# Linear heads of a hybrid decoder block: output kept with tokens on the partitions, then turned

## The reference

```python
# q_dec, a, v, s_prev: of one head; chunks n of 64 tokens
o = o_intra + jnp.einsum('bhnck,bhnkv->bhncv', q_dec, s_prev)      # o_intra = a @ v_c
o = o.transpose(0, 2, 3, 1, 4).reshape(bsz, s, A_HEADS, A_DV)      # 4 heads, 128 values each
o = o * lax.rsqrt(jnp.mean(o * o, axis=-1, keepdims=True) + EPS)   # per token and head
o = o.reshape(bsz, s, A_WIDTH) * norm_g.astype(f32) * jax.nn.silu(g.astype(f32))
```

## Time and profile before

| | us |
|---|---|
| median of 3 runs | 2257.88 (2255.01 to 2258.12) |
| the profiled execution | 2253.26 |
| its span in the trace | 2251.3 |
| PE busy | 2207.8 (98%), 11144 matmul instructions |
| DVE busy | 1438.0 (64%) |
| ACT busy | 1002.2 (45%) |
| POOL busy | 439.0 (19%) |

### The profile page before, as it was taken

One profiled execution on the slowest core, in us unless ns is written; L12 is line 12 of the kernel. 1 busy time (PEld: TensorE's weight loads), 2 busy tenths in 40 slices (PEclk: granted clock), 3 DMA queues, 4 the chain that ended last, 5 costly groups with the idle time before them and its releaser, 6 DMA issues.

```text
span 2251.3 us, 30000 instructions
## 1 busy us (share of the span) xinstructions
PE 2207.8 (98%) x11144; PEld 1840.7 (82%) x11144; DVE 1438.0 (64%) x2170; ACT 1002.2 (45%) x1717; POOL 439.0 (19%) x344
## 2 busy tenths in 40 slices
PE   7999999999999999999999999999999999999997
PEld 6888888888888888878888887888888888887886
DVE  5775577657776677675576765567665655555555
ACT  5554455445553554444433333346533333333444
POOL 1231022201220122032223331000222222210000
PEclk9999999999999999999999999999999999999999
DMA  4222333233233323633345656788443332327766
GB/s 124 92 76 71 117 113 94 95 103 119 74 122 99 113 62 107 207 112 114 117 171 200 223 199 211 255 268 264 163 145 103 101 110 99 112 77 237 229 206 215
DMA packets 260705, 321.81 MB, mean 143 GB/s; under 512 B 17232, under 2 KB 168784, under 8 KB 259536
## 3 DMA queue, kind: packets, MB, share of 16 engines
q1 hardware_dynamic: 259984, 317.79, 42.9%
q10 hardware_dynamic: 576, 2.10, 0.2%
HBM read 242.76 MB, written 77.07 MB: 142 GB/s over the span
## 4 chain that ended last, share of the span: by engine, by line
PE 91%; DVE 3%; DMA 2%; ACT 1%; issue 1%; SPq 0%; POOL 0%; DVEq 0%; ACTq 0%; POOLq 0%
PE M L1157 9%; PE M L1159 9%; PE M L1158 9%; PE M L850 8%; PE M L852 8%; PE M L851 8%; PE M L1184 3%; PE X L1184 3%; PE X L1186 3%; PE X L1185 3%; PE X L1159 3%; PE X L1157 3%; PE X L1158 3%; PE M L1186 3%; PE M L1185 3%; PE M L965 2%
## 5 line engine op out<-in xcount | busy, mean ns | idle before, releaser
L2139 DVE TENSOR_TENSOR ring_lo<-ring_raw,ring_hi 128x1024 fp32r<-128x1024 f32 x154 | 189.6, 1232 | 170.3 <-ACT ring_hi L1588 169.9
L1685 DVE TENSOR_TENSOR wlo<-raw,whi 128x1024 fp32r<-128x1024 f32 x120 | 154.6, 1288 | 213.6 <-ACT whi L1220 213.4
L850 PE MATMUL M<-uhi,whi 128*128 128x512 f32 (+1 forms) x720 | 285.2, 396 | 3.7 <-DVE wlo L1685 2.1
L852 PE MATMUL M<-uhi,wlo 128*128 128x512 f32 (+1 forms) x720 | 278.2, 386 | 0.0
L851 PE MATMUL M<-ulo,whi 128*128 128x512 f32 (+1 forms) x720 | 277.8, 386 | 0.0
L1588 ACT ACTIVATE ring_hi<-ring_raw 128x1024 fp32r<-128x1024 f32 x154 | 163.3, 1060 | 234.2 <-DMA ring_raw<-a_scr 230.8
L1157 PE MATMUL M<-t_hi,wu_hi 128*128 128x512 f32 x616 | 240.4, 390 | 4.1 <-DVE gq L2055 2.3
L1159 PE MATMUL M<-t_hi,wu_lo 128*128 128x512 f32 x616 | 240.0, 390 | 0.0
L1158 PE MATMUL M<-t_lo,wu_hi 128*128 128x512 f32 x616 | 239.7, 389 | 0.0
L1220 ACT ACTIVATE whi<-raw 128x1024 fp32r<-128x1024 f32 x120 | 126.8, 1056 | 220.7 <-PE M L852 170.0
L2023 DVE TENSOR_TENSOR wu_lo<-fraw,wu_hi 128x512 fp32r<-128x512 f32 x132 | 127.6, 975 | 120.1 <-ACT wu_hi L1529 119.8
(11 more groups left out here) (281 smaller groups left out, 5081.4 us busy)
## 6 DMA issues: line engine op xcount, KB each, us to landing
raw<-in_w_in_dram SPq DMA_DIRECT2D x88, 512.0 KB, 3.8
ring_raw<-a_scr SPq DMA_DIRECT2D x154, 256.0 KB, 3.5
fraw<-in_w_gate_dram SPq DMA_DIRECT2D x44, 512.0 KB, 4.4
fraw<-in_w_up_dram SPq DMA_DIRECT2D x44, 512.0 KB, 4.8
a_scr<-au SPq DMA_DIRECT2D x88, 256.0 KB, 2.3
ring_raw<-t_scr SPq DMA_DIRECT2D x88, 256.0 KB, 3.0
ring_raw<-in_w_down_dram SPq DMA_DIRECT2D x66, 256.0 KB, 3.0
raw<-in_w_out_dram SPq DMA_DIRECT2D x32, 512.0 KB, 3.8
```

The costliest lines, as they stand in the source:

```text
L850: mm(bank, whi[s][:, kb, :], hi, start=first, stop=False)
L852: return mm(bank, wlo[s][:, kb, :], hi, start=False, stop=last)
L1685: V.tensor_tensor(wlo[s][:, :, :], raw[s][:, :, :], whi[s][:, :, :].bitcast(F32), ALU.subtract).then_inc(s_lo[s], 1)
L2139: V.tensor_tensor(lo[:, :, :], raw_r[:, :, :], hi[:, :, :].bitcast(F32), ALU.subtract).then_inc(s_rowlo, 1)
```

## The change

The output is now made with tokens on the partitions. In OUTPUT the operands of all twelve products change places: `amask` and a 64-token piece of `qdec` are held, `iv` and the state are streamed. A chunk's product so writes 64 partitions by 128 columns, where it wrote 128 by 64. ACT squares X[2] in four pieces and sums each along the row into `oss`; the root and the reciprocal follow as before. DVE then multiplies X[2] by the reciprocal, spread along the row by its access pattern, into `sqo`, and this is now what reports `s_y1`. PE turns `sqo` into X[3] (`head_turn`, in the place of `head_mul`), and DVE multiplies X[3] by `ga` and the gate in one instruction. The sums of ones and the spreading by PE are gone, and so is the multiplication of X[2] by the gate in OUTPUT.

```diff
@@ PE
             def output(it, a):
                 for b in range(TB):
-                    mm(X[2][:, b * P:(b + 1) * P], iv[:, b * P:(b + 1) * P], amask[:, b, :],
+                    mm(X[2][:, b * P:(b + 1) * P], amask[:, b, :], iv[:, b * P:(b + 1) * P],
...
-                    last = mm(X[2][:, n * CHUNK:(n + 1) * CHUNK], before,
-                              qdec[a % 2][:, n * CHUNK:(n + 1) * CHUNK],
+                    b, c = divmod(n, 2)
+                    last = mm(X[2][CHUNK * c:CHUNK * c + CHUNK, b * P:(b + 1) * P],
+                              qdec[a % 2][:, n * CHUNK:(n + 1) * CHUNK], before,
-            def head_sum(it, a):
-                pe.wait_ge(s_sq, it * HEADS + a + 1)
-                pe.wait_ge(s_st, it * NCH * HEADS + NCH * a + NCH)
-                sums(X[3], sqo, s_asum)
-
-            def head_mul(it, a):
-                pe.wait_ge(s_arr, it * HEADS + a + 1)
-                spread(X[3], hrnrm, s_amul)
+            def head_turn(it, a):
+                pe.wait_ge(s_y1, it * HEADS + a + 1)
+                for b in range(TB):
+                    last = tr(X[3][:, b * P:(b + 1) * P], sqo[:, b * P:(b + 1) * P], ident[:, :])
+                last.then_inc(s_amul, 1)
@@ ACT
             def output(it, a):
                 act.wait_ge(s_o, it * HEADS + a + 1)
...
-                A(sqo[:, :], X[2][:, :], ACT.Square).then_inc(s_sq, 1)
+                for b in range(TB):
+                    tokens = slice(b * P, (b + 1) * P)
+                    A(sqo[:, tokens], X[2][:, tokens], ACT.Square, accum_out=oss[:, b:b + 1]).then_inc(s_sq, 1)
             def head_sum(it, a):
-                act.wait_ge(s_asum, it * HEADS + a + 1)
+                act.wait_ge(s_sq, (it * HEADS + a + 1) * TB)
...
-                A(hnrm[:, :], X[3][:, 0:TB], ACT.Sqrt, scale=1.0 / P, bias=epst[:, 0:1]).then_inc(s_aroot, 1)
+                A(hnrm[:, :], oss[:, :], ACT.Sqrt, scale=1.0 / P, bias=epst[:, 0:1]).then_inc(s_aroot, 1)
@@ DVE
-            def output(it, a):
-                n = it * HEADS + a
-                dve.wait_ge(s_sq, n + 1)
-                dve.wait_ge(s_gs, n + 1)
-                V.scalar_tensor_tensor(out=gate[a % 2][:, :], in0=X[2][:, :], scalar=ga[:, a:a + 1],
-                                       in1=gate[a % 2][:, :], op0=ALU.mult, op1=ALU.mult).then_inc(s_y1, 1)
             def head_sum(it, a):
                 dve.wait_ge(s_aroot, n + 1)
...
                 V.reciprocal(hrnrm[:, :], hnrm[:, :]).then_inc(s_arr, 1)
+                dve.wait_ge(s_arr, n + 1)
+                V.tensor_tensor(sqo[:, :].rearrange("p (b v) -> p b v", b=TB),
+                                X[2][:, :].rearrange("p (b v) -> p b v", b=TB),
+                                hrnrm[:, :].rearrange("p (b o) -> p b o", o=1).broadcast_to([P, TB, P]),
+                                ALU.mult).then_inc(s_y1, 1)
             def head_mul(it, a):
                 dve.wait_ge(s_amul, n + 1)
-                dve.wait_ge(s_y1, n + 1)
-                V.tensor_tensor(gate[a % 2][:, :], gate[a % 2][:, :], X[3][:, :], ALU.mult).then_inc(s_ya, 1)
+                dve.wait_ge(s_gs, n + 1)
+                V.scalar_tensor_tensor(out=gate[a % 2][:, :], in0=X[3][:, :], scalar=ga[:, a:a + 1],
+                                       in1=gate[a % 2][:, :], op0=ALU.mult, op1=ALU.mult).then_inc(s_ya, 1)
```

More of the change, by code:

```diff
@@ L251, in block_program @@
         nrm = sb("nrm", [P, TB]); rnrm = sb("rnrm", [P, TB])
-        hnrm = sb("hnrm", [P, TB]); hrnrm = sb("hrnrm", [P, TB])
+        oss = sb("oss", [P, TB]); hnrm = sb("hnrm", [P, TB]); hrnrm = sb("hrnrm", [P, TB])
         snrm = sb("snrm", [P, TB]); srnrm = sb("srnrm", [P, TB])
@@ L450, in block_program @@
         s_y1 = sem("s_y1")
-        s_asum = sem("s_asum")
         s_aroot = sem("s_aroot")
@@ L1079, in slots @@
                     if a is not None:
-                        head_mul(it, a)
+                        head_turn(it, a)
                     a = head_at(slot, UPDATE)
@@ L1095, in slots @@
                             step(it, i)
-                    for offset, step in ((KEYS, keys), (V_TURN, iv_turn), (UPDATE, update), (OUTPUT, output),
-                                         (NORM_SUM, head_sum)):
+                    for offset, step in ((KEYS, keys), (V_TURN, iv_turn), (UPDATE, update), (OUTPUT, output)):
                         a = head_at(slot, offset)
@@ L1275, in output @@
                 if a:
-                    act.wait_ge(s_asum, it * HEADS + a)
-                A(sqo[:, :], X[2][:, :], ACT.Square).then_inc(s_sq, 1)
+                    act.wait_ge(s_amul, it * HEADS + a)
+                    act.wait_ge(s_aroot, it * HEADS + a)
+                for b in range(TB):
+                    tokens = slice(b * P, (b + 1) * P)
+                    A(sqo[:, tokens], X[2][:, tokens], ACT.Square, accum_out=oss[:, b:b + 1]).then_inc(s_sq, 1)
             def head_sum(it, a):
-                act.wait_ge(s_asum, it * HEADS + a + 1)
+                act.wait_ge(s_sq, (it * HEADS + a + 1) * TB)
                 if a:
                     act.wait_ge(s_arr, it * HEADS + a)
-                A(hnrm[:, :], X[3][:, 0:TB], ACT.Sqrt, scale=1.0 / P, bias=epst[:, 0:1]).then_inc(s_aroot, 1)
+                A(hnrm[:, :], oss[:, :], ACT.Sqrt, scale=1.0 / P, bias=epst[:, 0:1]).then_inc(s_aroot, 1)
                 if it and a == 0:
@@ L1497, in op_hi @@
                     act.wait_ge(s_o, NSB * HEADS)
-                    act.wait_ge(s_asum, NSB * HEADS)
+                    act.wait_ge(s_amul, NSB * HEADS)
                     act.wait_ge(s_yalo, NSB * HEADS)
@@ L1819, in head_sum @@
                 if a:
-                    dve.wait_ge(s_amul, n)
+                    dve.wait_ge(s_y1, n)
                 V.reciprocal(hrnrm[:, :], hnrm[:, :]).then_inc(s_arr, 1)
+                dve.wait_ge(s_arr, n + 1)
[3 more added lines that the diff above has]
+                                ALU.mult).then_inc(s_y1, 1)
                 if it and a == 0:
@@ L1892, in slots @@
                         V.tensor_copy(oT[i // TB][:, :], M[3][:, :]).then_inc(s_oT, 1)
-                    for offset, step in ((KEYS, keys), (UPDATE, update), (OUTPUT, output), (NORM_SUM, head_sum)):
+                    for offset, step in ((KEYS, keys), (UPDATE, update), (NORM_SUM, head_sum)):
                         a = head_at(slot, offset)
```

## The result

| | before | changed |
|---|---|---|
| median of 4 runs, us | 2256.52 | 2239.19 (2238.90 to 2240.98) |
| ratio to before | | 0.9924, 95% interval 0.9912 to 0.9935 |
| profiled execution, us | 2253.26 | 2238.90 |
| span in the trace, us | 2251.3 | 2236.8 |

The changed kernel is 0.76% faster, 17.3 us in the medians; 2241.0 us were predicted, from a median before of 2257.88 us of three runs.

The account below looks back on a forecast made before the run. PE's issue stream was taken as the bound; 7.1 + 2.3 + 0.5 + 5.2 + 1.8 = 16.9 us kept of 30.9, giving 2241.0 us, 0.75% faster (forecast chance 0.69); range 2231 to 2252 us.

Parts of the forecast that it names:

- PE as the bound, and the stream's price: PE, busy 98% of the span, is the bound; each us out of its stream is gained if operands are ready.
- Chunk products: PE's 16 chunk products per head fall from 1.73 to 1.18 us, gaining 0.55; bounds 1.09 and 2.18 us.
- Rival A: Chunk products get no cheaper, staying at 108 ns each; the sum loses 8.8 us: 2250 us, chance 0.12.
- C: Rival: chunk products at 136 ns, 2.18 us instead of 1.18; 2257 us, no change that can be told, chance 0.09.
- D: Rival, slower: chunk products alternate between one bank's halves, each waiting for the one before; 2263 us at 158 ns, chance 0.06.
- The new wait at the heads 0 and 1: PE's transpose stands for DVE's product from 105.68 to about 106.75; 1.09 us given back, 0.89 kept per head.
- Rival B: The new wait never bites, DVE's product being ready when PE comes; 2227 us, chance 0.04.
- Head 2: The wait for DVE's product gives back all 1.43 us; kept 0.78 us in three blocks, 0.52 in the last.
- Head 3: No stall at the transpose, ACT's wait for PE's sums gone; kept 1.74 us three times, 1.79 once.
- 0.05 us for the turned inputs' DMA: Charge at head 3 in three blocks, for the turned input at 229.53 coming late behind DVE's `wlo`.
- What was hidden: ACT's square of 0.58 us becomes four, estimate 1.7 us; the 1.1 us more hide in ACT's idle time.
- The total: 16.9 us of 30.9 kept; span 2251.3 to 2234.4, profiled execution 2236.4, plus 4.6 for the median: 2241.0 us.

Follow-up runs that it names:

- sums_twice: Kernel before, with PE's four sums of squares by a column of ones made twice for every head; 2273.63 us, ratio 1.0060 to 1.0093.
- halves_early: Changed kernel, with SP's four loads of the second halves of x issued together before the first of the output weights; 2234.58 us.
- squares_twice: Changed kernel, with ACT's four squares with sums made twice; 2240.44 us.
- product_look: Same kernel as product_twice, run once more to trace an execution with a lower granted clock; 2250.83 us.
- product_twice: Changed kernel, with DVE's product of X[2] by the reciprocal made twice in a row, only the second reporting; 2251.07 us.
- product_thrice: Changed kernel, with DVE's product of X[2] by the reciprocal made three times; 2268.63 us.

## Why the prediction was right

**PE as the bound, and the stream's price.** Right. The mixers got 17.1 us shorter where the sum said 16.9, and sums_twice shows that a block of PE costs about what the chain says. How much of the 17.1 us is the change comes below.

**Chunk products.** That the form is cheaper was right, the size and the risk were not. The block went to 1.02 us, below the lower bound of 1.09. The prediction doubled the 0.59 us of the value products, and with them the 0.16 us that come once per block, and it took the change of halves for a risk. But the first product behind the block rose from 0.29 to 0.43 us in the chain, which the prediction had at nothing. Together 0.57 us in slot 9, where 0.55 was predicted: two errors of 0.14 to 0.16 us cancelled, which is luck. The second could have been read from the trace of before, behind its value products:

```profile
109.22 0.43 PE M L850
```

The weight load of this first product begins late. Before, it begins 0.06 us after the last chunk product of full width has begun; now 0.20 us after the last one that writes a half, with the loads standing for 0.17 us. The two loads, before and after:

```profile
93.02 0.19 PEld L850 LDWEIGHTS M<-uhi,whi 128*128 128x128 f32 x1
```
```profile
93.62 0.19 PEld L850 LDWEIGHTS M<-uhi,whi 128*128 128x128 f32 x1 [0.17 <-issue]
```

Rival A, to which the rule of the Trainium skill quoted in the prediction would have come, needed 1.73; C and D 2.18 and more.

**The new wait at the heads 0 and 1.** Right, with its cause: measured from the `whi` of slot 10, DVE's product ends at 107.33 - 99.40 = 7.93 us, and 106.71 - 98.81 = 7.90 was predicted. The transposes took 0.66 us, not 0.63. Kept 0.80 us per head against 0.89. The list gives 0.83 us of standing per head, not 1.07: it counts from the modelled end of the matmul before, 106.17 + 0.39 = 106.56, while the stream's pace of 0.23 us would have had the next one begin at 106.40. By these rows an earlier root wouldn't have helped much: it ended at 106.40, but DVE's `cuminv` only at 106.55. Rival B, by which this wait never bites, falls.

**Head 2.** Right in size in the blocks 0, 1 and 3: 0.84, 0.86 and 0.45 us kept, 0.78, 0.78 and 0.52 predicted. In block 0 also by its cause, the wait for `iv` that swallows what comes ahead of it. In block 1 this wait isn't there: the clock fell behind the wait for the product and cost about as much as `iv` would have. The waits in its slots, block 0 of the changed kernel:

```profile
191.45 0.66 PE L1029 MATMUL X<-ident,sqo 128*128 128x128 f32 x4 [1.25 <-DVE sqo L1816]
...
198.99 0.63 PE L999 MATMUL X<-ident,forget 128*128 128x128 f32 x4 [1.47 <-ACT iv L1262]
```

Block 2 kept 2.42 us, and 1.6 us of that no step of the sum had: in the trace of before the clock had fallen behind the wait for `iv`, and eight products took 0.43 us each in place of 0.23. The chain of before, in slot 22 of block 2:

```profile
676.25 0.63 PE X L999 x4
676.88 0.42 PE M L850
677.31 0.43 PE M L851
...
680.53 0.23 PE M L850
```

**Head 3.** Too high in the blocks 0 to 2: 1.34, 1.33 and 1.54 us kept, 1.74 predicted; in block 3 1.91 kept, 1.79 predicted. The term that failed is the 0.05 us for the turned inputs' DMA, charged in the first three blocks; 0.25 to 0.46 us were lost there. I had looked at the load of slot 26 only; the one of slot 25 is queued behind the load of weights that waits for the `wlo` of slot 24, and this moves up by slot 23's gain alone, while PE comes earlier by the sums and the transposes as well:

```profile
220.96 0.66 PE L1041 MATMUL X<-ident,xs 128*128 128x128 f32 x4 [0.97 <-DMA xs<-in_x_dram]
```

halves_early takes these waits away and gains 4 us.

**What was hidden.** Right. The four squares take some 1.0 us (0.25 us from one to the next), not 1.7, and squares_twice shows that twice as many still hide, but for the load just named.

**The total.** In the mixers 15.5 us came by the steps of the sum, 1.4 less than predicted, and 1.6 by a fall of the clock that the one trace of before happened to have where it cost its full price. The span was predicted at 2234.4 us and measured at 2236.8: 1.2 us are the late start and 1.4 the loss behind the mixers, less the 0.2 that the mixers gained beyond the sum. That the median came within 2 us all the same is in part luck. The prediction put 4.6 us on top of the profiled execution, but that of before happened to be a fast one; the changed kernel's median lies 0.3 us above its own. Over 33 later runs of before and the eight of the changed kernel the means are 2257.2 and 2238.5 us and the mean granted clocks 0.9964 and 0.9966, so on the average the falls cost both about the same. These means differ by 18.7 us; where the 3 us beyond the 15.5 lie, one trace of before can't tell.

## What to carry to other kernels

Where PE is full, an edit of its stream is worth the blocks of the chain; then lay the new operand's ready time beside PE's new, earlier arrival, with everyone's start taken from the group that releases them, and do it for each DMA behind a wait as well. A wait that is taken away uncovers the next one, so count the second-latest operand before naming a gain. Before scaling a block from a row of the chain, take two blocks of different length, so that what comes once per block isn't scaled too. Issue products into half the partitions so that both halves have work at the same time, and charge the first full-width product behind them.

## What the runs showed of the hardware

- Float32 products with 64 columns held, 128 streamed and all 128 rows in use: one instruction every 109 ns in each half of the output partitions, and the two halves run side by side when the order gives both work (0.01 us between the starts of a pair). A block of 16 took 1.02 us with the halves alternating at every product and 1.51 with one half after the other; a block of eight with the half changing at every second product took 0.59.
- The first full-width product behind such a block took 0.43 us in the chain, where 0.29 stood behind full-width ones; its weight load began 0.20 us after the last product of the block had begun, against 0.06.
- The granted clock fell to 1.2 GHz behind some stands of PE and not behind others like them. At head 2 a stand of 1.25 us had a fall behind it in 8 of 28 cases (seven traces), one of 1.97 us in 4 of 8 (product_look all, product_twice none), one of 2.7 us in 4 of 4. At the heads 0 and 1 stands of 0.83 and 1.55 us had none, those of 2.3 us 4 of 8. Mean granted clocks: 0.995 to 0.998 in the changed kernel and in before, 0.991 to 0.998 in product_twice and product_look, 0.989 in product_thrice.
- Such a fall cost 1.6 us where it could be read from the products (before, block 2), and less where a wait behind it would have come anyway. So a longer wait of PE can cost more than its length: 8.7 us of waits, less what `iv` swallowed, came out as 11.9 us in the medians.
- That the stand alone causes a fall isn't shown: at head 2 transposes and small products lie around it, and the same stand often has none behind it. One fall of sums_twice, at 827 us, has no wait ahead of it at all, only 16 instructions with a single column streamed each.
